# Sum of squares of seven norms: eight operands on TensorE in place of four pairs added by VectorE

## The reference

```
def rms_norm(x, w):
    y = xf * lax.rsqrt(jnp.mean(xf * xf, -1, keepdims=True) + RMS_EPS)
    return (y * w).astype(x.dtype)
hs = hs + keep * rms_norm(mix, norm_w[i, 1])
f = conv_ffn(rms_norm(hs, norm_w[i, 2]), ...)

def layer_norm(x, g, b):
    mu = xf.mean(-1, keepdims=True)
    var = jnp.mean(jnp.square(xf - mu), -1, keepdims=True)
    return (xf - mu) * lax.rsqrt(var + LN_EPS) * g + b
```

## Time and profile before

| | |
|---|---|
| time, median of 3 runs | 1666.21 us |
| the profiled execution's own time | 1672.88 us |
| its span, first to last instruction | 1671.1 us |
| TensorE matmul / weight load busy | 1519.6 / 1443.9 us |
| VectorE busy | 1068.0 us |
| ScalarE busy | 801.3 us |
| GpSimd busy | 252.8 us |
| mean granted TensorE clock | 0.932 |
| share of TensorE in the chain that ended last | 81% |

### The profile page before, as it was taken

The page is one execution under the profiler, slowest core; times in us unless marked ns, Lnnn a source line. Parts: engine busy times, 40 slices in busy tenths (PEclk is TensorE's granted clock), DMA queues, the critical chain, the costliest instruction groups (busy, mean ns, idle before and its releaser), DMA issues.

```text
span 1671.1 us, 32419 instructions
## 1 busy us (share of the span) xinstructions
PE 1519.6 (91%) x11621; PEld 1443.9 (86%) x11621; DVE 1068.0 (64%) x1785; ACT 801.3 (48%) x1389; POOL 252.8 (15%) x307
## 2 busy tenths in 40 slices
PE   6999969889999999878999988999999975899997
PEld 5997868789999989558999988989999954799996
DVE  4883956548885486336888456676664755576654
ACT  5555423436654364324655335454443652454443
POOL 0203001103552000000555000012110002011200
PEclk9999968999999999569999999999999985999998
DMA  5551310144555536103565534445555520255551
GB/s 200 178 175 63 115 39 1 52 141 133 181 174 180 159 114 191 36 3 99 178 183 177 172 108 139 140 148 180 186 177 176 180 89 1 88 165 180 184 179 61
DMA packets 61139, 222.51 MB, mean 133 GB/s; under 512 B 6784, under 2 KB 7808, under 8 KB 60672
## 3 DMA queue, kind: packets, MB, share of 16 engines
q1 hardware_dynamic: 60912, 220.17, 41.9%
q10 hardware_dynamic: 144, 1.18, 0.2%
HBM read 220.28 MB, written 1.05 MB: 132 GB/s over the span
## 4 chain that ended last, share of the span: by engine, by line
PE 81%; DVE 9%; ACT 5%; issue 3%; DMA 1%; POOL 0%; DVEq 0%; ACTq 0%; SPq 0%
PE bank L393 21%; PE bank L394 21%; PE bank L395 21%; PE bank L550 2%; PE bank L412 2%; PE bank L413 2%; ACT whi L369 2%; PE bank L1830 1%; DVE wlo L374 1%; PE bank L419 1%; PE bank L1204 1%; PE bank L1184 1%; DMA par<-params 1%; DVE work L1563 0%; PE bank L1232 0%
## 5 line engine op out<-in xcount | busy, mean ns | idle before, releaser
L374 DVE TENSOR_TENSOR wlo<-raw,whi 128x1024 fp32r<-128x1024 f32 x412 | 516.4, 1254 | 308.5 <-ACT whi L369 307.1
L369 ACT ACTIVATE whi<-raw 128x1024 fp32r<-128x1024 f32 x412 | 434.9, 1057 | 390.2 <-PE bank L395 371.0
L393 PE MATMUL bank<-xs,whi 128*128 128x272 f32 (+2 forms) x2080 | 598.5, 288 | 12.5 <-DVE wlo L374 10.8
L394 PE MATMUL bank<-xs,whi 128*128 128x272 f32 (+2 forms) x2080 | 595.4, 286 | 0.0
L395 PE MATMUL bank<-xs,wlo 128*128 128x272 f32 (+2 forms) x2080 | 593.1, 285 | 0.0
L393 PEld LDWEIGHTS bank<-xs,whi 128*128 128x128 f32 x2080 | 393.6, 189 | 16.5 <-issue 14.7
L395 PEld LDWEIGHTS bank<-xs,wlo 128*128 128x128 f32 x2080 | 394.6, 190 | 0.0
L394 PEld LDWEIGHTS bank<-xs,whi 128*128 128x128 f32 x2080 | 394.3, 190 | 0.0
L393 PE MATMUL bank<-hf,whi 128*128 (+2 forms) x1024 | 297.7, 291 | 11.8 <-issue 8.7
L394 PE MATMUL bank<-hf,whi 128*128 (+2 forms) x1024 | 294.6, 288 | 0.0
L395 PE MATMUL bank<-hf,wlo 128*128 (+2 forms) x1024 | 294.2, 287 | 0.0
(11 more groups left out here) (447 smaller groups left out, 1532.9 us busy)
## 6 DMA issues: line engine op xcount, KB each, us to landing
raw<-stream SPq DMA_DIRECT2D x412, 512.0 KB, 3.6
con<-consts SPq DMA_DIRECT2D x1, 1284.5 KB, 7.7
big<-mla ACTq DMA_DIRECT2D x1, 1152.0 KB, 5.0
hs_sb<-hs SPq DMA_DIRECT2D x1, 1088.0 KB, 5.0
y_out<-hs_sb SPq DMA_DIRECT2D x8, 128.0 KB, 2.1
par<-params SPq DMA_DIRECT2D x1, 644.0 KB, 8.8
```

Of the source, the lines that this page charges most:

```text
L369: nc.scalar.activation(whi[:, s, :], raw[:, s, :], ACT.Copy).then_inc(hi_split, 1)
L374: nc.vector.tensor_tensor(wlo[:, s, :], raw[:, s, :], whi[:, s, :].bitcast(F32), ALU.subtract).then_inc(block_split, 1)
L393: nc.tensor.matmul(out_, whi[:, slot, w], hi, start=start, stop=False)
L394: nc.tensor.matmul(out_, whi[:, slot, w], lo, start=False, stop=False)
```

## The change

`pair_sum` is taken out of VectorE's program in all seven norms (28 additions), and TensorE takes each of the eight squares by itself as soon as ScalarE has it: `meanwhile(k)` sums the square of operand k-1 from k = 1 on, and the last call takes operands 6 and 7. TensorE gets four more float32 products in each of the seven norms (28). The sums now wait for a mark of ScalarE, not of VectorE.

```
@@ -598,20 +598,14 @@
         dve.wait_ge(*v.at(f"{name}_y{m}"))
         nc.vector.tensor_tensor(hs[:, m, :], hs[:, m, :], y[:, m, :], ALU.add).then_inc(*v.mark(f"{name}_h{m}"))
 
-    def pair_sum(dve, name, m, T):
-
-        v = S("norm", "dve")
-        dve.wait_ge(*S("norm", "act").at(f"{name}_{m}"))
-        nc.vector.tensor_tensor(sq[:, m, 0:T], sq[:, m - 1, 0:T], sq[:, m, 0:T], ALU.add).then_inc(*v.mark(f"{name}_pair{m}"))
-
-    def pairs_in_wave(pe, name, g, T):
+    def squares_in_wave(pe, name, g, T):
 
         def src(m):
-            return "dve", f"{name}_pair{m}", sq[:, m, 0:T]
+            return "act", f"{name}_{m}", sq[:, m, 0:T]
 
         def meanwhile(k):
-            if k % 2 == 0 and k:
-                sums_pe(pe, name, src, g, ((k - 1, k == 2, False),), T)
+            if k:
+                sums_pe(pe, name, src, g, ((k - 1, k == 1, False),), T)
             if k == KC - 1:
                 sums_pe(pe, name, src, g, ((KC - 1, False, True),), T)
         return meanwhile
@@ -627,10 +621,7 @@
             add_y(dve, post, m)
             if m:
                 lo(m - 1)
-            if m % 2 == 0 and m:
-                pair_sum(dve, name, m - 1, T1)
         lo(KC - 1)
-        pair_sum(dve, name, KC - 1, T1)
         split_lo(dve, fourth(phase))
 
     def next_act(act, post, name, row, g, phase):
@@ -2008,11 +1999,8 @@
                 nc.vector.memset(w_bias[:, 0:1], 0.0).then_inc(bank_free, 1)
             if phase and m:
                 lo(m - 1)
-            if m % 2 == 0 and m:
-                pair_sum(dve, name + "v", m - 1, T2)
         if phase:
             lo(KC - 1)
-        pair_sum(dve, name + "v", KC - 1, T2)
         if phase:
             split_lo(dve, fourth(phase))
 
@@ -2861,8 +2849,8 @@
         gates_pe(pe, "gdn", G["gdn_g"], ((0, GROWS),), "gdn_gates", GROWS, T1, xk, lambda k: S("norm", "dve").at(f"pre0_x{k}"))
         pe_tiles(pe, "gdn_in", G["gdn_in"], "pre0", 32)
         gdn_pe(pe)
-        in_wave = lambda name: pairs_in_wave(pe, name, G[name], T1)
-        ln_wave = lambda n: pairs_in_wave(pe, f"ln{n}v", G[f"lv{n}"], T2)
+        in_wave = lambda name: squares_in_wave(pe, name, G[name], T1)
+        ln_wave = lambda n: squares_in_wave(pe, f"ln{n}v", G[f"lv{n}"], T2)
         pe_wide(pe, "gdn_out", G["gdn_out"], mix_ready("gdn"), gdn_banks_read, post_in_row(pe, "post0", G["post0"]))
         post_pe(pe, "post0", G["post0"])
         pe_tiles(pe, "up0", G["up0"], "pre1", None, in_wave("pre1"))
```

## The result

The change makes the kernel slower, as forecast: 1677.89 us (median of 4 runs, 1677.59 to 1679.06) against 1666.12 us before, ratio 1.0070 with a 95% interval of 1.0052 to 1.0087. The forecast was 1675.1 us, so +8.9 us by the sum against 11.8 us by the medians. The time lies in the whole range (1671 to 1679) and slightly above the forecast's own of 1673 to 1677.5.

A forecast was written before the change was run, and what follows sets the result against it. The prediction took TensorE to bound the six waves and VectorE's pairs to be on the last norm's path. 5.5 + 5.2 - 1.8 = +8.9 us on the 1666.21 us median gave 1675.1 us, own range 1673 to 1677.5, whole range 1671 to 1679.

The forecast's parts named there:

- The waves are bound by TensorE, nothing hides a sum.: In the six waves TensorE is busy throughout and VectorE runs ahead, so added sums lengthen them by their whole cost.
- One comparison in the working: Inside a wave, TensorE at 1.36 us an operand was called slower than VectorE at 1.24 or 1.60 us.
- 12 x 0.46 + 12 x 0.43 = 10.7 us: Cost of four more sums in each of three 272-token and three 256-token waves, added to TensorE's time.
- The trace against the page: A 128x272 sum costs 0.46 us by the trace, 0.23 us by the skill page, which would make about +2.7 us overall.
- The sums at full clock, no wait for the squares of ScalarE, the pause behind the wave unchanged: In the waves, added sums follow the half-clock head and wait for no square; the 1.37 us pause behind stays.
- The last norm gives back 1.8 us: In the last norm, where pairs are on the path, the root starts 1.8 us earlier, at full clock.
- The same difference lands on the median: Whole kernel: +8.9 us on the profiled 1672.88 us carries over to the unprofiled median 1666.21 us, giving 1675.1 us.
- The rivals on the clock: Half-clock stretches at root-mean-square norms fall away (1668.3 us, 4%), or one enters the three layer-norm waves (up to 1680.2 us, 6%).
- six stretches at half clock: Two at each of three root-mean-square norms, 3.4 us each; any other number would show the forecast wrong.
- VectorE's time counts after all: The waves follow VectorE, whose freed 10.3 us counts with the last norm's 1.8 us: 1654 us, 2%.

The follow-up runs named there:

- Run 4: Kernel before without VectorE's pair additions, TensorE summing only operands 1, 3, 5 and 7, so half of each norm's sum is missing: 1665.55 us, ratio 0.9988.
- the quick run of before: The kernel before, unedited, traced once more: its profiled execution took 1665.75 us, against a median of 1666.96 us on that chip.
- late sums: Kernel before with 24 extra sums in one wave, the one behind ln2: 1676.48 us, ratio 1.0049.
- all sums early: Kernel before with 24 extra sums in the first wave, behind post0: 1675.99 us, ratio 1.0047.
- runs 7 and 10: The change repeated with more runs: 1681.24 us; the change with rounded squares and one-pass sums in the seven norms: 1660.51 us, ratio 0.9945 to the kernel before.

## Why the prediction was right, and by how much it was off

- *The waves are bound by TensorE, nothing hides a sum.* Right, and shown from four corners: waves of 12.3 to 12.5 and 10.5 us with four sums, 14.1 to 14.4 and 12.2 with eight, whether VectorE adds pairs or not. Two waves of 15.3 and 15.4 us had over 2 us more of half clock. One comparison in the working doesn't hold: behind post0 TensorE's 1.36 us for an operand was less than VectorE's mean of 1.42 (1.24 and 1.60 in turn), so TensorE was not the slower one by pace. It still had no wait. The 3.4 us of half clock at the wave's head cost it about 1.7 us by an estimate, and that lead of VectorE outlasts the 0.5 us that it loses over eight operands. Run 4 shows that a quicker VectorE buys nothing there.
- *12 x 0.46 + 12 x 0.43 = 10.7 us.* Right: the six waves of the change are 10.7 us longer than those of the quick run of before. 24 sums at one place gave 0.45 and 0.43 us each.
- *The trace against the page.* The Trainium skill (Perfetto Trace Analysis, Engine Utilization) halves TensorE's output rate for FP32_LOW_HIGH; by an estimate from that a sum of 128x272 would take 0.23 us. The traces have 0.46 us. Whether these products are of that kind no run shows, and the measurement decides.
- *The sums at full clock, no wait for the squares of ScalarE, the pause behind the wave unchanged.* Right: the first sum behind post0 starts at 379.7 us, where the clock had been full since 378.9, the waves of the change have no wait in them, and the pause is 1.37 us in both.
- *The last norm gives back 1.8 us.* Measured 1.7 us against the trace that it was worked out from (6.47 to 4.81), 1.95 us against the quick one, at full clock in the change. I had TensorE start 0.1 us too early after the first square, and the 0.3 to 0.6 us of clock in the gain were not in the working as such.
- *The same difference lands on the median.* This is the step that was off. I took 1672.88 against 1666.21 us for the profiler's cost and carried the sum over. It was the clock: the trace was of a slow execution of the kernel before. The sum of instruction costs didn't suffer from it, but the clock's term did: I let it be nil, with the chance of a few microseconds spread on both sides (4% and 6%), and between a quick execution of before and one of the change it was +3.3 us. That it landed within 3 us of the median was partly luck: by pairs of traces the same +8.9 was 3.9 us too much (first trace of before) and 3.2 us too little (quick one).
- *The rivals on the clock.* Both came in part, mostly at places that neither named. Of the six stretches at half clock one fell away in the change's first trace, that ahead of the wave behind post1, and with it one at post3, which I hadn't counted; each gave back 1.4 us. So the stretches were five and not six, which the prediction had named as a sign of being wrong: its assumption that the clock would repeat its pattern failed there. Half clock was added in the odd mixer (58.0 us in place of 47.8, and the segment 5.1 us longer, half of the 10.2) and in the mLSTM segment (68.7 in place of 61.7, and 1.3 us longer), not in the layer-norm waves, which stayed at 1.00. I had named the waves as the place because I looked only where the change puts work.
- *VectorE's time counts after all.* Fell: run 4 takes it away and no wave shrinks.

What stays open: why the clock in the odd mixer comes back 10 us later in the change. In every trace with the original or late sums its segment was one of two lengths (147.8 us or 152.3 us), in the traces with eight float32 sums in the waves 151.5 to 153.0 us, with one-pass sums 149.5 and 150.0 us, with all sums early 148.8 us. That it depends on when the mixer's bursts of matmuls come is a guess: no run moved that alone, and one kernel showed both lengths without any edit. Nor is it shown how often the change has each pattern, since only two traces of it exist.

## What to carry to other kernels

Moving a reduction's additions from an idle engine to the matrix engine pays only where the matrix engine waits for them: here in one norm of seven. Price it at what one operation costs in the busy engine's own chain; a float32 sum cost three and a half split matmuls, and making it one pass, with rounded squares, turned +13.5 us into -7.2 (runs 7 and 10, medians on one chip). Before a trace is used as a baseline, compare its own time and mean clock with the median of the runs: a difference may be the execution's and not the profiler's.

## What was not expected of the hardware

- The same instructions of the odd mixer took 147.88 us at a mean clock of 0.84 and 152.31 us at 0.80, in two executions of one kernel; the two kinds of execution are 1665.75 and 1673.03 us.
- The odd mixer had 58.0 us of half clock in both traces of the change, where it starts 5 to 7 us later than in the quick run of before with 47.8 us; but the two slow traces of before had 61.4 us with no edit. Two traces of the change can't tell a steady effect of the shift from chance.
- The profiler cost nothing that can be seen: a profiled execution took 1665.75 us where the median on that chip was 1666.96.
